# Router logits tile by tile, a first gather without the route tables, and tables and weights made beside it

## The reference

```python
logits = (hf @ w_router).astype(jnp.float32) + b_router.astype(jnp.float32)   # 512 x 32
top_v, top_i = lax.top_k(logits, TOP_K)                                       # 4 of 32 experts
top_w = jax.nn.softmax(top_v, axis=-1)
...
gu = xb @ w_gate_up[e] + b_gate_up[e]        # per block of rows of one expert e
gate = jnp.minimum(gu[:, :D_EXPERT], SWIGLU_LIMIT)
up = jnp.clip(gu[:, D_EXPERT:], -SWIGLU_LIMIT, SWIGLU_LIMIT)
glu = gate * jax.nn.sigmoid(SWIGLU_ALPHA * gate)
return ((up + 1.0) * glu) @ w_down[e] + b_down[e]
```

## Time and profile before

| | |
|---|---|
| median of 3 runs | 2174.62 us (2172.08 to 2175.55) |
| the profiled execution's own time | 2170.76 us |
| its span, first to last instruction | 2168.6 us |
| busy in the span | PE 95%, DVE 40%, ACT 21%, POOL 17% |
| mean granted TensorE clock | 0.974 of full speed |
| transfers | 520.47 MB, mean 240 GB/s; over 400 GB/s in most of the expert loop |

### The profile page before, as it was taken

How to read it: one execution, slowest core, us unless ns; L and a number is a source line. 1 busy time by engine, 2 the same in 40 slices (tenths; PEclk the granted TensorE clock), 3 DMA queues, 4 the chain that set the end, 5 groups by cost and what they waited for, 6 DMA issues and landing times.

```text
span 2168.6 us, 41783 instructions
## 1 busy us (share of the span) xinstructions
PE 2055.2 (95%) x17356; PEld 1276.6 (59%) x17356; DVE 865.3 (40%) x1472; ACT 456.8 (21%) x737; POOL 359.7 (17%) x389
## 2 busy tenths in 40 slices
PE   6999898599999999999999999988999998999998
PEld 5888666135444544443543443437776777888887
DVE  4454434433233333323332332324566443444444
ACT  4251433000000000000000000014454532212221
POOL 1010000112222232222223222232201200000000
PEclk9999998799999999999999999988999999999999
DMA  6334113899999999999999999973211021233231
GB/s 238 110 121 135 59 39 126 341 347 408 405 406 402 411 404 404 410 402 401 403 406 400 404 407 397 402 271 113 68 59 39 1 78 59 80 111 100 78 112 42
DMA packets 157311, 520.47 MB, mean 240 GB/s; under 512 B 16412, under 2 KB 71760, under 8 KB 124400
## 3 DMA queue, kind: packets, MB, share of 16 engines
q1 hardware_dynamic: 136480, 494.96, 58.4%
q0 software_dynamic: 20784, 24.85, 4.8%
HBM read 509.61 MB, written 18.88 MB: 244 GB/s over the span
## 4 chain that ended last, share of the span: by engine, by line
PE 62%; SPq 7%; DMA 5%; DVE 3%; issue 1%; POOL 1%; ACT 1%; ACTq 0%; DVEq 0%; POOLq 0%
PE ps L1974 23%; PE ps L1988 11%; PE ps L392 8%; PE ps L394 8%; PE ps L393 8%; SPq L567 4%; DMA ring_a<-in_w_gate_up 4%; SPq L569 3%; PE ps L1883 2%; DMA ring_a<-in_w_down 1%; POOL rstd L466 1%; PE ps L494 1%; PE ps L1893 1%; PE ps L1875 1%; PE ps L1836 0%
## 5 line engine op out<-in xcount | busy, mean ns | idle before, releaser
L1974 PE MATMUL ps<-ring_a,xe 128*32 128x512 f32 x3912 | 438.9, 598 | 11.9 <-DVE xe L1585 10.3
L1988 PE MATMUL ps<-ring_a,act_t 128*32 128x256 f32 x6000 | 334.7, 379 | 5.3 <-DMA ring_a<-in_w_down 3.6
L1974 PEld LDWEIGHTS ps<-ring_a,xe 128*32 128x32 f32 x3912 | 130.1, 111 | 293.3 <-issue 253.5
L1988 PEld LDWEIGHTS ps<-ring_a,act_t 128*32 128x32 f32 x6000 | 219.0, 110 | 128.3 <-issue 21.9
L1974 PE MATMUL ps<-ring_b,xe 128*32 128x512 f32 x2232 | 253.1, 594 | 0.0
L392 PE MATMUL ps<-xt_hi,hi 128*128 128x512 f32 x576 | 227.9, 396 | 5.6 <-DVE xt_lo L507 4.7
L394 PE MATMUL ps<-xt_hi,lo 128*128 128x512 f32 x576 | 225.6, 392 | 0.0
L393 PE MATMUL ps<-xt_lo,hi 128*128 128x512 f32 x576 | 225.4, 391 | 0.0
L1076 ACT ACTIVATE glu<-glu 128x768 f32<-128x768 f32 x32 | 27.0, 845 | 660.6 <-DVE glu L1592 598.8
L1974 PEld LDWEIGHTS ps<-ring_b,xe 128*32 128x32 f32 x2232 | 77.6, 110 | 142.0 <-issue 133.4
L759 POOL DMA_INDIRECT x_rows<-ye,idx x96 | 154.4, 1608 | 37.9 <-issue 37.9
(11 more groups left out here) (297 smaller groups left out, 2418.1 us busy)
## 6 DMA issues: line engine op xcount, KB each, us to landing
ring_a<-in_w_gate_up SPq DMA_DIRECT2D x163, 1024.0 KB
ring_a<-in_w_down SPq DMA_DIRECT2D x125, 1024.0 KB
ring_b<-in_w_gate_up SPq DMA_DIRECT2D x93, 1024.0 KB
raw<-in_w_in SPq DMA_DIRECT2D x20, 1024.0 KB, 8.1
raw<-in_w_gate SPq DMA_DIRECT2D x11, 1024.0 KB, 5.3
raw<-in_w_up SPq DMA_DIRECT2D x11, 1024.0 KB, 5.4
raw<-in_w_down SPq DMA_DIRECT2D x11, 1024.0 KB, 4.9
raw<-in_w_out SPq DMA_DIRECT2D x8, 1024.0 KB, 5.0
```

What stands on the lines that cost most here:

```text
L1974: last = pe.matmul(ps[QUAD * j:QUAD * j + QUAD, g, :], xe[:, g, QUAD * k:QUAD * k + QUAD], w[:, j, :, :, :], start=k == 0, stop=k == KT - 1)
L1988: last = pe.matmul(y_block(g, j), act_t[:, g, QUAD * (2 * c + h):QUAD * (2 * c + h) + QUAD], w[:, h, QF * j:QF * j + QF], start=c == 0 and ...
```

## The change

1. The router's logits are made one tile at a time (`router_logits`): 8 slices, two matmuls each, on 128 tokens. `wr_hi` and `wr_lo` now lie side by side in `wr_s`, so that one matmul with 64 stationary columns gives `hi` x `xt_hi` on partitions 0 to 31 and `lo` x `xt_hi` on 32 to 63; a second, with 32 columns, adds `hi` x `xt_lo`. Tile 0 stands between the norm transposes of tiles 2 and 3, tiles 1 to 3 behind those of tile 3. They write to the banks of the last chunk. ACT copies each tile to `lgT` (64 x 128), and four matmuls against a constant take the place of the transposes and add the two halves.
2. `posm` keeps position plus one; the first 32 columns of `posx` are made at once, and `select(0)` reads them and `dst` itself. `n_blk` (`route_counts`) is made while PE sums the slots, the rest of `posx` and all of `dstx` (`route_tables`) behind the first `idx`.
3. `route_weights` and `select(1)` now stand ahead of the first `x_transpose`; `indices(1)`, `pick_row(1)` and the second `x_transpose` ahead of `swiglu(0)`.
4. POOL clears `xg` once the logits are made and issues the first gather without `r_table`; DVE, PE and POOL read `n_blk` later. SP's wait for the logits counts four tiles.

```diff
-            sp.wait_ge(r_lgT, 1)
+            sp.wait_ge(r_lgT, T)
...
         def moe_moves(pool):
-            pool.wait_ge(r_table, 1)
+            pool.wait_ge(r_lgT, T)
...
+            gather(pool, 0, 0)
+            pool.wait_ge(r_table, 1)
             n1 = pool.value_load(n_blk[0:1, 0:1], min_val=NE - 1, max_val=MAXB - 1)
-            gather(pool, 0, 0)
             gather(pool, 1, 1)
...
+            def logits_copy(t):
+                act.wait_ge(r_lgT, t + 1)
+                copy(lgT[:, t * P:(t + 1) * P], logits_bank(t)[:, 0:P]).then_inc(r_lgT_sb, 1)
...
                     norm_hi(act, NS[name] + t, tile(xt_hi, t))
+                    if logits and t == 2:
+                        logits_copy(0)
+                if logits:
+                    for t in range(1, T):
+                        logits_copy(t)
...
-            act.wait_ge(r_lgT, 1)
-            copy(lgT[:, :], ps[0:NE, 5, :]).then_inc(r_lgT_sb, 1)
...
-            link(dve.tensor_scalar(posm[:, :, :], posm[:, :, :], 1.0, None, ALU.subtract))
-            for q in range(PASSES):
-                dve.tensor_scalar(posx[:, :, NE * q:NE * q + NE], posm[:, :, :], float(CAP * q), None, ALU.subtract)
-                dve.tensor_copy(dstx[:, :, NE * q:NE * q + NE], dst[:, :, :])
-            dve.memset(posx[:, :, MAXB:MAXB + 1], -1.0)
-            dve.memset(dstx[:, :, MAXB:MAXB + 1], 0.0)
+            link(dve.tensor_scalar(posx[:, :, 0:NE], posm[:, :, :], 1.0, None, ALU.subtract))
+
+        def route_counts(dve, link):
...
+        def route_tables(dve, link):
+            for q in range(1, PASSES):
+                dve.tensor_scalar(posx[:, :, NE * q:NE * q + NE], posm[:, :, :], float(CAP * q + 1), None, ALU.subtract)
+            for q in range(PASSES):
+                dve.tensor_copy(dstx[:, :, NE * q:NE * q + NE], dst[:, :, :])
...
         def moe_vector(dve, link_route):
-            dve.wait_ge(r_table, 1)
-            n1 = dve.value_load(n_blk[0:1, 0:1], min_val=NE - 1, max_val=MAXB - 1)
...
-            select(0, None)
+            select(0, None, dst)
+            route_counts(dve, link_route)
             indices(0, None, None, parts=1)
+            route_tables(dve, link_route)
             pick_row(0, None)
-            x_transpose(0, None)
+            dve.wait_ge(r_table, 1)
+            n1 = dve.value_load(n_blk[0:1, 0:1], min_val=NE - 1, max_val=MAXB - 1)
             route_weights(dve, link_route)
             select(1, 0)
+            x_transpose(0, None)
             indices(1, None, 48)
+            pick_row(1, 1)
+            x_transpose(1, 8)
             swiglu(0, 8)
-            pick_row(1, 8)
-            x_transpose(1, 8)
             act_transpose(0, 8)
...
-            pe.wait_ge(r_wlo, 1)
-            for k in range(KT):
-                last = split3(pe, ps[0:NE, 5, :], wr_hi[:, k, :], wr_lo[:, k, :], xt_hi[:, k, :], xt_lo[:, k, :],
-                              k == 0, k == KT - 1)
-            last.then_inc(r_lgT, 1)
-            pe.wait_ge(r_lgT_sb, 1)
+            pe.wait_ge(r_lgT_sb, T)
             for t in range(T):
-                last = pe.transpose(ps[:, 4, NE * t:NE * t + NE], lgT[:, t * P:(t + 1) * P], ident[0:NE, 0:NE])
+                last = mm(ps[:, 4, NE * t:NE * t + NE], lgT[:, t * P:(t + 1) * P], const[0:2 * NE, C_OWN:C_OWN + NE],
+                          start=True, stop=True, skip_group_check=True)
             last.then_inc(r_done, 1)
...
+        def router_logits(pe, t):
+            pe.wait_ge(n_lo, NS["ffn"] + t + 1)
+            evacuated(pe, SA, SA.first[A_END - 1] + t)
+            pe.wait_ge(r_wlo, 1)
+            o = logits_bank(t)
+            for k in range(KT):
+                pe.matmul(o[:, 0:P], wr_s[:, k, :], xt_hi[:, k, t * P:(t + 1) * P], start=k == 0, stop=False,
+                          skip_group_check=True)
+                last = pe.matmul(o[0:NE, 0:P], wr_hi[:, k, :], xt_lo[:, k, t * P:(t + 1) * P], start=False,
+                                 stop=k == KT - 1, skip_group_check=True)
+            last.then_inc(r_lgT, 1)
...
             transpose(T - 2)
+            if name == "ffn":
+                router_logits(pe, 0)
             transpose(T - 1)
+            if name == "ffn":
+                for t in range(1, T):
+                    router_logits(pe, t)
```

More of the change, by code:

```diff
@@ L198, in program @@
         wr = at("wr", K(0), [P, KT, NE])
-        wr_hi = at("wr_hi", K(1), [P, KT, NE], F32R)
-        wr_lo = at("wr_lo", K(2), [P, KT, NE], F32R)
+        wr_s = at("wr_s", K(1), [P, KT, 2 * NE], F32R)
+        wr_hi, wr_lo = wr_s[:, :, 0:NE], wr_s[:, :, NE:2 * NE]
         lg = at("lg", K(3), [P, T, NE])
-        lgT = at("lgT", K(28), [NE, SEQ])
+        lgT = at("lgT", K(28), [2 * NE, SEQ])
         top_v = at("top_v", K(32), [P, T, 8])
@@ L896, in scalar_program @@
             act.wait_ge(r_in, 16)
-            copy(wr_hi[:, :, :], wr[:, :, :]).then_inc(r_hi, 1)
-            norm_behind_chunk("ffn", SA, A_END - 1)
-            act.wait_ge(r_lgT, 1)
-            copy(lgT[:, :], ps[0:NE, 5, :]).then_inc(r_lgT_sb, 1)
+            copy(wr_hi, wr[:, :, :]).then_inc(r_hi, 1)
+            norm_behind_chunk("ffn", SA, A_END - 1, logits=True)
             act.wait_ge(r_sub, 1)
@@ L1040, in scalar_program, with logits_bank @@
             ffn_scalar(act)
+        def logits_bank(t):
+            return ps[0:2 * NE, SA.bank(SA.first[A_END - 1] + t), :]
         BD_ORDER = (0, 2, 3, 1)
@@ L1265, in vector_program @@
             dve.wait_ge(r_hi, 1)
-            dve.tensor_tensor(wr_lo[:, :, :], wr[:, :, :], wr_hi[:, :, :].bitcast(F32), ALU.subtract).then_inc(r_wlo, 1)
+            dve.tensor_tensor(wr_lo, wr[:, :, :], wr_hi.bitcast(F32), ALU.subtract).then_inc(r_wlo, 1)
             dve.wait_ge(gain_in[1], 32)
@@ L1502, in route @@
             dve.tensor_scalar(n_blk[:, 1:2], cnt[:, 6:7], float(NE - 2), None, ALU.add).then_inc(r_table, 1)
+        def route_tables(dve, link):
[3 more added lines that the diff above has]
+                dve.tensor_copy(dstx[:, :, NE * q:NE * q + NE], dst[:, :, :])
+            dve.memset(posx[:, :, MAXB:MAXB + 1], -1.0)
+            link(dve.memset(dstx[:, :, MAXB:MAXB + 1], 0.0))
         def route_weights(dve, link):
@@ L1530, in link, with select @@
                 dve.wait_ge(moe_dve_step, base_[0] + steps[0])
-            def select(n, before):
+            def select(n, before, rows_of=dstx):
                 dve.wait_ge(m_pos, n)
                 for t in range(T):
-                    i = dve.tensor_scalar(sel[:, t, :], cc(C_SLOT, CAP), posx[:, t, bass.ds(n, 1)], dstx[:, t, bass.ds(n, 1)],
+                    i = dve.tensor_scalar(sel[:, t, :], cc(C_SLOT, CAP), posx[:, t, bass.ds(n, 1)], rows_of[:, t, bass.ds(n, 1)],
                                           ALU.is_equal, ALU.mult)
@@ L1940, in chunk_and_norm @@
             transpose(T - 2)
+            if name == "ffn":
+                router_logits(pe, 0)
             transpose(T - 1)
+            if name == "ffn":
+                for t in range(1, T):
+                    router_logits(pe, t)
             pe.wait_ge(n_lo, s + T)
         def moe_tensor(pe):
-            pe.wait_ge(r_table, 1)
-            n1 = pe.value_load(n_blk[0:1, 0:1], min_val=NE - 1, max_val=MAXB - 1)
             def slot_sums(n, parts=2):
@@ L1993, in moe_tensor @@
             slot_sums(0, 1)
+            pe.wait_ge(r_table, 1)
+            n1 = pe.value_load(n_blk[0:1, 0:1], min_val=NE - 1, max_val=MAXB - 1)
             pe.wait_ge(b_top, 3)
```

2 lines of the change are left out of this document (1 added, 1 removed).

## The result

The changed kernel takes 2159.96 us (median of 5 runs, 2157.32 to 2163.82), the kernel before 2172.75 beside it (2170.22 to 2175.55): a ratio of 0.9937, 95% interval 0.9925 to 0.9949, or 12.8 us less. 1.9 us of the distance to 2167.5 is the kernel before itself, whose median was 2174.62 when the forecast was made; 5.7 us is the sum.

A forecast was written before the change was run, and what follows sets the result against it. It took PE's start of blocks 0 and 1 to bound the loop, with no slack in PE or transfers. -2.7 - 3.3 + 1.4 - 0.6 - 1.9 = -7.1 us gave 2167.5 us against the median; range 2164.5 to 2171.5.

The forecast's parts named there:

- the sum: All terms together: -7.1 us, from the profiled 2170.76 to 2163.7, or 2167.5 against the median of the runs.
- What bounds the kernel: Expert loop: PE and transfers balanced without slack, so starting PE's first chunks earlier brings the whole loop forward about equally.
- Part 1: Router to DVE's first step: narrow matmuls -3.0, shorter copy -0.3, matmuls replacing the transposes +0.6; -2.7 us.
- Part 2: First list made without the tables, counts and `n_blk` load ahead of it: -3.3 us.
- Part 3: From list to first `xe`: moved DVE work, not the gather, holds `xe`, +1.4 us.
- the second `own_q`: Block 0: PE no longer waits 0.64 us for it, -0.6 us.
- Part 4: Seam between blocks 0 and 1: gap shrinks from 4.74 to 2.85 us, -1.9; clock still falls, 0.
- (a): Rival: the clock stays up in the seam, giving back 2.6 us; -9.7 in all, 2164.9; chance 0.14.
- (b): Rival: DVE's work stretches POOL's first gather issues, +2.3 us; sum -4.8, 2169.8; chance 0.13.
- (c): Rival: narrow router matmuls cost what wide ones do; no gain from 0.25 us each; chance 0.19, 0.08 of it slower.
- Behind the loop: Stages after the expert loop: nothing changes, they only start earlier; 0 us.

The follow-up runs named there:

- The doubled price: The changed kernel with each tile's 16 router matmuls made twice, the first pass overwritten: 2167.29 us in one execution.
- the early `xe`: The changed kernel with unread matmuls ahead of both blocks, first `x_transpose` ahead of `select(1)`, second slot sums two chunks later: 2157.09 us, 0.9921.
- the freed late router: The changed kernel with all four tiles' narrow logits matmuls behind the last transposes and ACT's tile 0 copy moved behind too: 2161.29 us, one execution.
- the same order undone: The changed kernel with `swiglu(0)` again ahead of the second `pick_row` and `x_transpose`: 2161.03 us, 0.9940.
- both runs with the late router: The changed kernel with all narrow logits matmuls behind the last transposes, ACT's tile 0 copy kept early or moved too: 2163.51 and 2161.29 us.
- the second comparison: The changed kernel run once more beside the kernel before on the same chip: 2161.63 us, 0.9931.

## Why the forecast was right in its path and wrong in its size

**What bounds the kernel: right.** Every stage that came earlier brought the rest earlier. From block 1's `act_t` to the loop's end it is 974.0 us before and 973.3 after, and the DMA share where the ring had stood still is 1.01.

**Part 1, the router: the step that failed.** -7.4 us instead of -2.7 in the profiled pair, two thirds of the miss and more, in two terms.

The larger is the price of a narrow matmul. "I take the middle, 0.175 us at 1.2 GHz and about half, 0.095": it is 0.107 and 0.060. The forecast divided the wide router's 8.46 us by 24, which mixes both levels of the clock, and then went halfway to the transposes, whose 1.94 us hold a tail, and which start 0.21 us apart at the half clock (after's trace), twice the price of the narrow matmul with the same 128 columns. The trace of before had the price in the starts of the wide matmuls, four of which are these (PE's timeline, two at the half clock and two at the full):

```profile
371.63 0.63 PE L393 MATMUL ps<-xt_lo,wr_hi 128*32 128x512 f32 x1
372.05 0.63 PE L394 MATMUL ps<-xt_hi,wr_lo 128*32 128x512 f32 x1
...
377.42 0.39 PE L392 MATMUL ps<-xt_hi,wr_hi 128*32 128x512 f32 x1
377.65 0.39 PE L393 MATMUL ps<-xt_lo,wr_hi 128*32 128x512 f32 x1
```

0.42 us and 0.23 us from start to start for 512 columns; a quarter is 0.106 and 0.058. The forecast had the quarter as its lower bound, and even that (0.09) was an average of the two levels.

The Trainium skill, "TensorE: Matmul & The Clock Gate", section "Back-to-back issue gap", gives two figures for 128 columns: about 81 ns in a stream of weight loads and matmuls, and for a matmul by itself 128 / 1.2 = 107 ns at the half clock and 128 / 2.4 + 2.5 = 56 ns at the full one. The runs show 107 and 60 ns, in a stream with a weight load ahead of each matmul (32 or 64 stationary columns). So the second figure bears on this kernel; the forecast had weighed only the first, whose estimate for the router's end, 375.8, is 4.2 us late (371.39 + 0.22). The sum that goes with that end is -8.0, not -7.8: 0.9 us below -7.1.

The smaller term is the clock. The forecast let tile 0, tile 3's transposes and tile 1 run at 1.2 GHz, up to 373.65, and had tile 3 delayed by 2.0 us. The clock was granted in full from about 366.5, while tile 0 was being made, and there was no delay. The doubled price shows this term by itself: 1.5 us of the miss; the rest, 3.2, is the price. That split is of these executions: in the second one of the changed kernel the half clock lasted until 371.4, tile 3's remainder came 0.7 us later than before, counted from tile 2's transposes, and Part 1 was -6.0 to -6.2 (10.43 against 16.40 and 16.64). Even there the clock rose sooner and the delay was shorter than the forecast had it. With both terms right, what is left behind tile 3's remainder is 16 matmuls, 0.95 us, and not 3.6 (373.1 to 376.7). The copies and the four matmuls against the constant were as said.

**Part 2: right,** -3.5 for -3.3, and the same to 0.02 us in every kernel with either order.

**Part 3: right in its mechanism, by a narrow margin,** +0.85 for +1.4. DVE's order and not the gather held `xe` in the profiled run, by 0.3 to 0.55 us as the early `xe` shows. In the freed late router, with the same order on DVE, `xe` did wait for the gather, 11.17 us behind the list: the two ends lie so close that it was partly luck which one came last. Block 0 itself gained 0.9 where 0.6 was said for the second `own_q`; how long the half clock lasts in its first chunks varies (6.86 to 8.25 us for the first 48 without added matmuls), and the forecast had left that open.

**Part 4: right in the gap** (1.8 for 1.9), **wrong in "0" for the clock.** The clock fell again, as forecast, but the first 24 matmuls took 4.24 us, not 5.35. With the same order undone it was 4.07 behind the long gap, so that this isn't set by the gap alone.

**The rivals.** (a) did not happen in the profiled run of after, but it is real: in both runs with the late router the clock stayed up across a seam of the same code, and `act_t` to `act_t` took 30.21 us; it fell in the four other runs with that seam and no added matmuls. What decides was not found. (b) did not happen: the three issues took 1.13, 1.03 and 1.05 us with DVE's tables and weights beside them, against 1.13, 1.03 and 1.00 before, the last in the earlier trace rows. The rule of the Trainium skill, "SBUF — State Buffer", section "Who interferes with whom", is not seen at work there; the neighbours were copies and operations of 0.3 us. (c) was far off: 0.060 to 0.107 us against the 0.25 from which it would have decided.

**Behind the loop:** 0 was right on the average and not in the profiled pair. The stages up to the loop's end gave 14.7 us, the medians 12.8 and, in the second comparison, 13.5; the stretch from tile 2's transposes to the loop's end is 1080.7 and 1080.1 us in the two executions of before and 1066.3 and 1066.9 in the two of after, 13.8 us.

## What to carry to other kernels

Price a new matmul shape by the start-to-start distance of the nearest one, at one level of the clock at a time and in proportion to its moving columns; durations overlap, and a group's mean mixes the levels. When work on a chain is cut into pieces behind a producer that delivers in pieces, count only the last piece and ask whether the others fit into the producer's own time: if they do, their price no longer matters, and if they nearly do, it decides everything. And where a few microseconds are compared between two profiled runs, first take the stages whose code is the same in both: they show how much two executions differ by themselves. One trace of each kernel doesn't: the same router took 9.25 us in one execution and 10.43 in the next.

## What the runs showed of the hardware

- The clock's fall and rise don't follow from the code alone. Tile 2's transposes of the kernel before took 1.94 us in one execution and 1.06 in another, tile 3's of the changed kernel 1.04 and 1.91, and the same seam ran at the full clock in two executions and fell in four.
- The clock falls in an idle stretch or some time behind it. In the changed kernel's seam it was 1.00 in the 2.55 idle microseconds and 0.67 in the 3.4 us behind them; in the norm of the same trace, with PE idle from 361.1 to 363.90, it was 0.87 from 362.6 to 363.4 and 0.50 from there on, before PE went on. With matmuls that nobody reads, 1.99 us of them in the seam's gap, it stayed at 1.00 there in all three executions; without them, in two of six.
- At half clock the first two or three chunks of a block are paced by PE, not by their transfers: 72 matmuls took 7.93 us with the clock up, where 48 took 7.47.
